# Slot tables filled tile by tile, and expert rows added to the tokens' rows by accumulating scatters, in an encoder layer with 64 experts

## The chip, the cores and the metric

The kernel runs on one core of a Trainium2 chip. The metric is the device time of one execution in microseconds (us), lower is better. The kernel before took 1889.31 us (median of 3 runs, 1889.1 to 1889.86). The execution that the profiler recorded took 1872.73 us, of which 1870.9 us are its span.

## What is computed

One encoder layer on 1024 tokens of width 1024, float32. After the token mixers (a state-space scan and attention, whose outputs are `[s ; a]`), and with alpha = 2^0.25:

```
x1  = LN(alpha * x + [s ; a] @ W_o)
scores = sigmoid(x1 @ w_router); top 6 of 64 experts per token (within the best 4 of 8 groups)
w   = scores of the six / their sum * 2.5
f   = sum over the six of w * ((silu(x1 @ Wg[e]) * (x1 @ Wu[e])) @ Wd[e])  +  the shared expert of x1
out = LN(alpha * x1 + f)
```

Each expert has width 256, so its three weight matrices are 1 MB each. An expert's tokens are handled in blocks of 128 slots. There are 64 main blocks, one per expert, and overflow blocks for experts with more than 128 tokens (here one: the blocks run 65 times).

## The kernel before, in words

The stages run one after another, each in a block with a barrier of all engines behind it. The change touches the last four.

**Mix stage** (`mix_norm_route`, L1022, from 797.9 us of the span). Eight tiles t of 128 tokens. TensorE (PE) makes `[s;a] @ W_o` (L1109, L1114) two tiles ahead, turns x1 (L1123), and makes the router's logits (L1134) and the ranks of the tokens within their experts (L1141, L1143). VectorE (DVE) does the LayerNorm (L1210 to L1223), copies half of the turned x1 (L1265), keeps the ranks (L1259) and picks the experts (L1228 to L1255). SyncE's queue (SP) zeroes the overflow part of `y_d` (24 MB, L1081) and stores x1 rows. The first half of the shared expert's gate and up products (L1005) fills PE's end of the stage.

**Dispatch stage** (`dispatch`, L1292, from about 980 us). DVE computes the overflow blocks and the slot of each of the 8 x 6 x 128 assignments (L1332 to L1358). GpSimd (POOL) then scatters the token numbers with 48 indirect DMAs (L1379) into `slot_tok_d` in memory. SP reads the table back (L1393), PE turns it (L1412), and DVE writes the slot table `block_tok` (L1370). Beside it PE does the shared expert's remaining products (L1005, L1407), DVE adds them to alpha * x1 in `k.x` (L1368), and the first three experts' weights are loaded (ACT's queue, L1322).

**Expert stage** (`moe_experts`, L1422). For each block, in program order on each engine:

- POOL: `gather(e)` copies four index columns (L1485), waits for that copy, and issues four indirect DMAs, one per quarter row (L1489), into one of two `xg` buffers. It waits only for `turn_x(e-2)` (L1497).
- DVE, iteration i: `turn_x(i+2)` (L1614), `hidden(i+1)` (L1619, L1621), `keep_y(i)` (L1631), `keep_hT(i+1)` (L1625).
- PE: `gate_up(c+1)` (L1516), `down(c)` (L1536), `turn_h(c+1)` (L1524).
- ACT: sigmoid (L1572), the other half of `keep_y` (L1578), and the plain store of the block's 128 rows to `y_d` (L1581).
- SP: the three weight loads of expert e+4 when `down(e)` has ended (L1014 to L1016).

**Combine stage** (`combine`, L1672). For each tile POOL gathers six rows per token from `y_d` (L1710, 48 indirect DMAs of 128 rows of 4 KB). Four of them are weighted and added by PE (L1724) and two by DVE (L1755). DVE adds PE's sum (L1758) and does the whole LayerNorm (L1760 to L1770), and SP stores the tile.

The order of the DVE loop is what the prediction leans on:

```
for ii, u:  i = ii * 2 + u
    turn_x(i + 2, u, ...); hidden(i + 1, 1 - u); keep_y(i, u, ...); keep_hT(i + 1, 1 - u)
```

Of the kernel before, what the change touches and what calls it, by code (L numbers as in the profile page):

```python
# [13 lines left out]
P = 128  # L14
# [119 lines left out]
def persistent(nc, ctx, k):  # L134
# [28 lines left out]
    k.y_d = nc.dram_tensor("y_d", (SLOTS, D), f32).ap()  # L163
    k.slot_tok_d = nc.dram_tensor("slot_tok_d", (SLOTS, 1), f32).ap()
# [857 lines left out]
def mix_norm_route(nc, k):  # L1022

    with ExitStack() as ctx:
# [4 lines left out]
        zeros = sb("zeros", [P, D], f32)  # L1029
# [21 lines left out]
        hots = sb("hots", [P, TOP_K, N_EXPERTS], f32)  # L1051
        wsum = sb("wsum", [P, 1], f32)
# [11 lines left out]
        zeroed, y_zeroed = sem("zeroed"), sem("y_zeroed")  # L1064
# [9 lines left out]
        def _(sp):  # L1074
# [16 lines left out]
        def _(pe):
# [34 lines left out]
            def route(t):  # L1126
                pe.wait_ge(xT_dve, t + 1)
# [22 lines left out]
            mix(1)  # L1150
            for t in range(T):
# [8 lines left out]
                if t + 2 >= T:  # L1160

                    n = t + 2 - T
                    pe.wait_ge(mix_read, 2 * t + 2)
                    if n == 0:
                        pe.wait_ge(k.ws_in, 48)
                    shared_gate_up(nc, k, n, p_m[:, n, :]).then_inc(gu_done, 1)
            pe.wait_ge(rank_read, T - 1)
            rank(T - 1)

            pe.wait_ge(rank_read, T)  # L1170
            pe.wait_ge(member_done, T + 1)
# [30 lines left out]
        def _(dve):  # L1202
# [60 lines left out]
            for t in range(T):  # L1263
# [4 lines left out]
                if t:  # L1268
                    keep_rank(t - 1)
# [146 lines left out]

def moe_experts(nc, k):  # L1422
# [423 lines left out]
```

## Time and profile before

| | us |
|---|---|
| median of 3 runs | 1889.31 |
| profiled execution | 1872.73 |
| its span | 1870.9 |
| mixers, up to the mix stage | 798 |
| mix stage | 798 to 980 |
| dispatch stage | 980 to 1059 |
| expert stage | 1059 to 1779 |
| combine stage | 1779 to 1871 |

PE is busy in 87% of the span, DVE in 49%, POOL in 19%, ACT in 18%. Times in rows are microseconds from the span's start, durations are microseconds unless marked ns. A row of the timeline gives start, duration, engine, line, operation, written tile and read tiles, the count, and in brackets the idle time of the engine before it with what ended it. PEclk is TensorE's granted clock as a share of 2.4 GHz.

### The profile page before, as it was taken

How to read it: one execution, taken by the hardware profiler on the slowest of the kernel's cores; microseconds unless marked ns; L12 is line 12 of the kernel's file. 1: busy time of each engine (PE TensorE's matmuls, PEld its weight loads, DVE VectorE, ACT ScalarE, POOL GpSimd, SP SyncE). 2: the span in 40 equal slices, each digit the busy share in tenths (PEclk: the TensorE clock that was granted, in tenths of full speed). 3: DMA queues.
4: the chain of work that ended last, by engine and by line, in shares of the span. 5: the costliest groups of instructions: out<-in, count | busy, mean ns of one | idle time of the engine just before them, and what ended most of it. 6: DMA issues, size and time to landing. Idle time of an engine off the chain costs nothing. (4 is left out here: it accounts for less than half of the span.)

```text
span 1870.9 us, 18631 instructions
## 1 busy us (share of the span) xinstructions
PE 1620.8 (87%) x6004; PEld 929.7 (50%) x6004; DVE 911.0 (49%) x1664; ACT 342.8 (18%) x616; POOL 355.8 (19%) x425
## 2 busy tenths in 40 slices
PE   7989999999665664699989299999999999999775
PEld 4556777777564554245544144444444444444232
DVE  1553444445698884537866133333333333333168
ACT  1303443443412330112200000010100000010010
POOL 0000000000000000000006543333434343343073
PEclk9988999999866666799989699999999999999988
DMA  8010000000411113695008269999999999999296
GB/s 223 12 41 4 4 4 5 5 0 1 42 16 22 19 15 62 230 372 241 35 15 201 97 252 400 401 398 396 395 407 399 394 396 406 397 395 398 104 377 274
DMA packets 117211, 367.34 MB, mean 196 GB/s; under 512 B 38594, under 2 KB 55090, under 8 KB 92210
## 3 DMA queue, kind: packets, MB, share of 16 engines
q1 hardware_dynamic: 84434, 264.00, 39.0%
q0 software_dynamic: 20928, 59.29, 8.1%
q10 hardware_dynamic: 11808, 43.53, 6.6%
q8 instruction: 23, 0.38, 0.1%
q14 instruction: 18, 0.15, 0.0%
HBM read 292.76 MB, written 71.91 MB: 195 GB/s over the span
## 5 line engine op out<-in xcount | busy, mean ns | idle before, releaser
L1516 PE MATMUL moe_p_gu<-ring_gu,moe_xgT 128*128 128x512 f32 x784 | 348.4, 598 | 18.9 <-DVE moe_xgT L1614 18.9
L1489 POOL DMA_INDIRECT moe_xg<-x_d,moe_idx x260 | 247.2, 951 | 114.4 <-issue 63.2
L1516 PEld LDWEIGHTS moe_p_gu<-ring_gu,moe_xgT 128*128 128x128 f32 x784 | 146.9, 192 | 186.4 <-issue 171.1
L1379 POOL DMA_INDIRECT slot_tok_d<-all_const,all_dest_i x48 | 46.5, 970 | 1003.9 <-DVE all_dest_i L1358 989.6
L1536 PE MATMUL moe_p_y<-ring_dn,moe_hT 128*128 128x512 f32 x392 | 176.3, 592 | 0.8 <-DVE moe_hT L1625 0.8
L1619 DVE TENSOR_TENSOR moe_gs<-moe_sig,moe_p_gu 128x256 f32<-128x256 f32 x65 | 27.4, 421 | 303.4 <-ACT moe_sig L1572 303.4
L1614 DVE STREAM_TRANSPOSE moe_xgT<-moe_xg 128x1024 f32<-128x1024 f32 x65 | 131.2, 2020 | 13.0 <-DMA moe_xg<-x_d,moe_idx 11.9
L1572 ACT ACTIVATE moe_sig<-moe_p_gu 128x256 f32<-128x256 f32 x65 | 25.0, 384 | 600.3 <-PE moe_p_gu L1516 600.3
L583 PEld LDWEIGHTS att_p_o<-att_v,att_prT 128*128 128x128 f32 x1024 | 120.4, 192 | 19.5 <-issue 17.6
L583 PE MATMUL att_p_o<-att_v,att_prT 128*128 128x64 f32 x1024 | 123.7, 274 | 1.5 <-DVE att_prT L660 1.5
L530 PE MATMUL att_p_s<-latents_kT,att_qT 96*128 96x512 f32 x256 | 123.6, 607 | 0.0
L646 DVE TENSOR_REDUCE att_nmax<-att_p_s 128x1 f32<-128x1024 f32 x64 | 78.4, 1225 | 92.7 <-PE att_p_s L530 92.4
L1536 PEld LDWEIGHTS moe_p_y<-ring_dn,moe_hT 128*128 128x128 f32 x392 | 74.4, 190 | 94.2 <-issue 94.2
L1631 DVE COPY moe_y<-moe_p_y 128x512 f32<-128x512 f32 x65 | 45.0, 692 | 145.6 <-PE moe_p_y L1536 145.6
L1516 PE MATMUL moe_p_gu<-moe_gu,moe_xgT 128*128 128x512 f32 x256 | 112.5, 592 | 0.0
L753 PE MATMUL ssm_p_v<-ssm_U,ssm_w_in 128*128 x256 | 56.4, 414 | 45.4 <-DVE ssm_gsn L860 31.3
L1724 PE MATMUL comb_p_sum<-comb_yb,comb_diag 128*128 128x512 f32 x128 | 58.7, 613 | 25.0 <-DMA comb_yb<-y_d,all_dest_i 25.0
L753 PEld LDWEIGHTS ssm_p_v<-ssm_U,ssm_w_in 128*128 128x128 f32 x256 | 53.3, 320 | 49.9 <-DVE ssm_gsn L860 34.2
L1516 PEld LDWEIGHTS moe_p_gu<-moe_gu,moe_xgT 128*128 128x128 f32 x256 | 47.5, 191 | 53.6 <-issue 53.6
L616 ACT ACTIVATE att_pr<-att_p_s,att_bias 128x1024 f32<-128x1024 f32 x64 | 71.0, 1110 | 3.1 <-DVE att_bias L647 3.1
L1485 POOL COPY moe_idx<-ring_block_tok 128x4 int32 (+1 forms) x65 | 12.1, 185 | 299.4 <-DVE moe_xgT L1614 291.3
L569 PE MATMUL att_p_t<-all_const,att_pr 128*128 128x128 f32 x512 | 66.9, 274 | 0.0
(319 smaller groups left out, 2178.5 us busy)
## 6 DMA issues: line engine op xcount, KB each, us to landing
ring_gu<-in_we_gate_dram SPq DMA_DIRECT2D x46, 1024.0 KB, 7.9
ring_gu<-in_we_up_dram SPq DMA_DIRECT2D x46, 1024.0 KB, 11.2
ring_dn<-in_we_down_dram SPq DMA_DIRECT2D x46, 1024.0 KB, 13.8
y_d<-moe_y ACTq DMA_DIRECT2D x65, 512.0 KB, 9.3
y_d<-mix_zeros SPq DMA_DIRECT2D x1, 24576.0 KB, 66.2
moe_gu<-in_we_gate_dram SPq DMA_DIRECT2D x16, 1024.0 KB, 8.0
moe_gu<-in_we_up_dram SPq DMA_DIRECT2D x16, 1024.0 KB, 11.3
moe_dn<-in_we_down_dram SPq DMA_DIRECT2D x16, 1024.0 KB, 13.8
```

The costliest lines, as they stand in the source:

```text
L530: last = nc.tensor.matmul(p_s[:, t % 2, half * 512:(half + 1) * 512], qT[:, u, t * P:(t + 1) * P], kT[:, u, half * 512:(half + 1) * 512], ...
L569: last = nc.tensor.transpose(p_t[:, j, :], pr[:, t % 2, j * P:(j + 1) * P], k.ident)
L583: last = nc.tensor.matmul(p_o[:, 0:DV], prT[:, t % 2, j, :], v[:, u, j, :], start=(j == 0), stop=(j == T - 1))
L616: nc.scalar.activation(pr[:, t % 2, :], p_s[:, t % 2, :], ACT.Exp, bias=bias[:, t % 2:t % 2 + 1], scale=SCALE, accum_out=total[:, t % 4:t ...
L646: ch.link(nc.vector.tensor_reduce(nmax[:, t % 2:t % 2 + 1], p_s[:, t % 2, :], AX.X, ALU.max, negate=True))
L753: last = nc.tensor.matmul(p_v[:, x % 2, part, r, :], w_in[:, gd, part * N:part * N + P], U[:, bass.ds(b * GB + half * 4 + r, 1), :].rearra ...
L1379: nc.gpsimd.indirect_dma_start(k.slot_tok_d[:, :], bass.IndirectOffsetOnAxis(ap=k.dest[:, t * TOP_K + q:t * TOP_K + q + 1], axis=0), k.tok ...
L1489: nc.gpsimd.indirect_dma_start(xg[:, u, g, :], None, x1_quarters, bass.IndirectOffsetOnAxis(ap=idx[:, u, g:g + 1], axis=0)).then_inc(xg_in ...
L1516: last = nc.tensor.matmul(p_gu[:, u, :], xgT[:, u, kk, :], k.moe_gu[v][:, :, kk * F:(kk + 1) * F], start=(kk == 0), stop=(kk == KD - 1))
L1536: last = nc.tensor.matmul(p_y[:, half * 512:(half + 1) * 512], hT[:, u, kk, :], k.moe_dn[v][:, kk * D + half * 512:kk * D + (half + 1) * 512],
L1614: nc.vector.transpose(xgT[:, u].rearrange("p k (g i) -> p g k i", g=NQ), xg[:, u].rearrange("p g (j k) -> p g k j", k=KD)).then_inc(x_turn ...
L1724: last = nc.tensor.matmul(p_sum[:, t % 2, cols], diag[:, t % 2, q, :], yb[:, n % NB, cols], start=(q == 0), stop=(q == PE_K - 1))
```

## The change

- **Slots.** A slot is now (level, expert, place): level = rank // 128 takes the place of the compacted overflow number, so a tile's destinations (`place(t)`) are known as soon as its ranks are. They are scattered in the mix stage, tile by tile, as entries of three numbers: token for the gather, token for the scatter, weight. Unfilled slots hold token number 1024 + place and weight 0.
- **Mix stage.** POOL adds the LayerNorm's bias (`shift`) and issues the 48 scatters. ACT copies the whole turned x1. All four parts of the shared expert's gate and up products are made here. The stage ends with the tables' way back: 64 blocks by a plain load, the 48 overflow blocks by an indirect one, then six transposes.
- **No dispatch stage.** The shared expert's down products and the sum with alpha * x1 move to the start of the expert stage, and SP stores the sums to `sum_d`.
- **Expert stage.** POOL copies three small tables per block, gathers with a bounds check, and issues for each block one indirect DMA that adds the 128 weighted rows (4 KB each) to `sum_d`. It does so once the block's rows are in `y` and the scatter before it has landed. The weighting is in the two copies from PSUM.
- **Combine stage.** Eight plain loads of `sum_d`, statistics, normalisation on ACT, scale on DVE, bias on POOL, store.

The diff, cut to its core:

```diff
@@ mix_norm_route
+            def shift(t):
+                pool.wait_ge(scaled, t + 1)
+                nc.gpsimd.tensor_tensor(k.x[:, t, :], r[:, :], b1[:, :], ALU.add).then_inc(x1_done, 1)
+            def scatter(t):
+                pool.wait_ge(dest_done, t + 1)
+                for q in range(TOP_K):
+                    n = t * TOP_K + q
+                    nc.gpsimd.indirect_dma_start(k.slot_d[:, :], bass.IndirectOffsetOnAxis(ap=k.dest[:, n:n + 1], axis=0),
+                                                 k.entry[:, t, q, :], None).then_inc(scattered, 16)
...
             for t in range(T):
                 turn_x(t)
                 if t + 3 < T:
                     turn_o(t + 3)
                 if t + 2 < T:
                     mix(t + 2)
+                else:
+                    pe.wait_ge(mix_read, 2 * t + 2)
+                    shared(t + 2 - T)
                 if t:
                     rank(t - 1)
                 route(t)
+            shared(2)
             pe.wait_ge(rank_read, T - 1)
             rank(T - 1)
...
+            shared(3)
+            pe.wait_ge(main_in, 16)
+            pe.wait_ge(over_in, 16)
...
+            def place(t):
                 dve.wait_ge(ranked, t + 1)
-                nc.vector.tensor_copy(k.rank[:, t, :], p_rank).then_inc(rank_read, 1)
+                nc.vector.tensor_tensor(hots[:, :, :], hot[:, :, :], p_rank.unsqueeze(1).to_broadcast([P, TOP_K, N_EXPERTS]),
+                                        ALU.mult).then_inc(rank_read, 1)
+                dve.wait_ge(rank_read, t + 1)
+                ch.link(nc.vector.tensor_reduce(rank[:, :], hots[:, :, :], AX.X, ALU.add))
...
             for t in range(T):
-                dve.wait_ge(x_turned, 2 * t + 1)
-                nc.vector.tensor_copy(k.x1T[:, 0:4, t * P:(t + 1) * P], p_x[:, 0:4, :]).then_inc(xT_dve, 1)
                 if t + 1 < T:
                     norm(t + 1)
                 if t:
-                    keep_rank(t - 1)
+                    place(t - 1)
                 route(t)
@@ moe_experts
+            for t in range(T):
+                sp.wait_ge(s_read, 2 * t + 2)
+                sp.dma_start(k.sum_d[t * P:(t + 1) * P, :], k.x[:, t, :]).then_inc(sum_out, 16)
...
+            def gather(n, col, u, c, free=None):
+                if free is not None:
+                    pool.wait_ge(x_turned, free)
+                nc.gpsimd.tensor_copy(dst[:, c, :], k.block_dst[:, bass.ds(col, 1)]).then_inc(idx_done, 1)
+                nc.gpsimd.tensor_copy(wgt[:, c, :], k.block_w[:, bass.ds(col, 1)]).then_inc(idx_done, 1)
+                nc.gpsimd.tensor_copy(idx[:, u, :], k.block_tok[:, bass.ds(col, 1), :].rearrange("p b g -> p (b g)")).then_inc(idx_done, 1)
+                pool.wait_ge(idx_done, n * 3 + 3)
                 pool.sem_inc(idx_seen, 1)
                 for g in range(NQ):
                     nc.gpsimd.indirect_dma_start(xg[:, u, g, :], None, x1_quarters,
-                                                 bass.IndirectOffsetOnAxis(ap=idx[:, u, g:g + 1], axis=0)).then_inc(xg_in[u], 16)
+                                                 bass.IndirectOffsetOnAxis(ap=idx[:, u, g:g + 1], axis=0),
+                                                 bounds_check=NQ * SEQ - 1, oob_is_err=False).then_inc(xg_in[u], 16)
+            def scatter(n, u, c, first=False):
+                pool.wait_ge(y_act, n + 1)
+                pool.wait_ge(y_dve, n + 1)
+                if not first:
+                    pool.wait_ge(y_out, n * 16)
+                pool.sem_inc(y_taken, 1)
+                nc.gpsimd.indirect_dma_start(k.sum_d[:, :], bass.IndirectOffsetOnAxis(ap=dst[:, c, :], axis=0),
+                                             y[:, u, :], None, compute_op=ALU.add).then_inc(y_out, 16)
...
+            gather(2, OVER + 2, 0, 2, free=1)
+            pool.wait_ge(sum_out, 16 * T)
+            scatter(0, 0, 0, first=True)
+            gather(3, OVER + 3, 1, 3, free=2)
+            scatter(1, 1, 1)
+            with pool.Fori(0, E // 4 - 1) as ee:
+                for v in range(4):
+                    e = ee * 4 + v
+                    gather(e + 4, ee * 4 + (OVER + 4 + v), v % 2, v, free=e + 3)
+                    scatter(e + 2, v % 2, (v + 2) % 4)
...
-            def keep_y(e, u, n):
+            def keep_y(e, u, c, sent=True):
                 dve.wait_ge(y_done, e * 2 + 2)
-                if n is not None:
-                    dve.wait_ge(y_out[u], n)
-                nc.vector.tensor_copy(y[:, u, 512:D], p_y[:, 512:D]).then_inc(y_dve, 1)
+                if sent:
+                    dve.wait_ge(y_out, e * 16 - 16)
+                nc.vector.tensor_scalar(y[:, u, 512:D], p_y[:, 512:D], wgt[:, c, :], None, ALU.mult).then_inc(y_dve, 1)
...
-            with dve.Fori(1, E // 2 - 1) as ii:
-                for u in range(2):
-                    i = ii * 2 + u
-                    turn_x(i + 2, u, ii * LANDED + 2 * LANDED, i + 1)
+            with dve.Fori(0, E // 4 - 1) as ii:
+                for v in range(4):
+                    i, u = ii * 4 + v + 2, v % 2
+                    turn_x(i + 2, u, ii * (2 * LANDED) + (v // 2 + 3) * LANDED, i + 1)
                     hidden(i + 1, 1 - u)
-                    keep_y(i, u, ii * 16)
+                    keep_y(i, u, (v + 2) % 4)
                     keep_hT(i + 1, 1 - u)
@@ combine
+            for t in range(T):
+                sp.dma_start(k.x[:, t, :], k.sum_d[t * P:(t + 1) * P, :]).then_inc(x_in[t], 16)
...
+                nc.gpsimd.tensor_tensor(xn[:, t, :], xn[:, t, :], b2[:, :], ALU.add).then_inc(out_done, 1)
...
+                nc.scalar.activation(xn[:, t, :], k.x[:, t, :], ACT.Identity, bias=nbias[:, t:t + 1], scale=rstd[:, t:t + 1]).then_inc(normed, 1)
```

## Rows read from the trace of the kernel before

**Rows 1.** Busy time by stretch: start:end, length, then each engine's busy time, clock, DMA.

```profile
1250.00:1350.00 100.00, 100.00 (x249) 45.55 (x248) 37.17 (x48) 9.43 (x19) 36.24 (x47) 1.00 1.01 399
```

**Rows 2.** The timeline of one expert block in the steady part.

```profile
1304.47 7.03 PE L1516 MATMUL moe_p_gu<-ring_gu,moe_xgT 128*128 128x512 f32 x16
1304.53 0.69 DVE L1631 COPY moe_y<-moe_p_y 128x512 f32<-128x512 f32 x1 [2.23 <-PE moe_p_y L1536]
1305.47 2.02 DVE L1614 STREAM_TRANSPOSE moe_xgT<-moe_xg 128x1024 f32<-128x1024 f32 x1
1307.66 0.18 POOL L1485 COPY moe_idx<-ring_block_tok 128x4 int32 x1 [4.93 <-DVE moe_xgT L1614]
1308.63 0.97 POOL L1489 DMA_INDIRECT moe_xg<-x_d,moe_idx  x1 [0.79 <-POOL moe_idx L1485]
1309.90 0.95 POOL L1489 DMA_INDIRECT moe_xg<-x_d,moe_idx  x1 [0.30 <-issue]
1311.34 3.60 PE L1536 MATMUL moe_p_y<-ring_dn,moe_hT 128*128 128x512 f32 x8
1311.95 0.42 DVE L1619 TENSOR_TENSOR moe_gs<-moe_sig,moe_p_gu 128x256 f32<-128x256 f32 x1 [4.46 <-ACT moe_sig L1572]
1312.41 0.42 DVE L1621 TENSOR_TENSOR moe_h<-moe_gs,moe_p_gu 128x256 f32<-128x256 f32 x1
```

**Rows 3.** Tile moe_xg, 1250 to 1350 us: from a gather's issue to its landing.

```profile
DMA to landing us min/median/max: 4.9/6.3/7.1
```

**Rows 4.** Tile moe_xg, 1080 to 1095 us, when few other transfers run.

```profile
DMA to landing us min/median/max: 2.7/2.8/2.9
```

**Rows 5.** DMA over 1150 to 1700 us: bytes and rate.

```profile
DMA packets 40082, 219.05 MB, mean 398 GB/s; under 512 B 6668, under 2 KB 6668, under 8 KB 20024
```

**Rows 6.** DMA issues: KB each, median us to landing (1730 to 1780; 1780 to 1871).

```profile
y_d<-moe_y ACTq DMA_DIRECT2D x4, 512.0 KB, 2.6
comb_yb<-y_d,all_dest_i POOLq DMA_INDIRECT x48, 9.1
```

**Rows 7.** Timeline: expert stage, first product, first and last copies of its chain, end.

```profile
1072.56 9.07 PE L1516 MATMUL moe_p_gu<-ring_gu,moe_xgT 128*128 128x512 f32 x16 [15.02 <-DVE moe_xgT L1614]
1093.86 0.69 DVE L1631 COPY moe_y<-moe_p_y 128x512 f32<-128x512 f32 x1 [2.14 <-PE moe_p_y L1536]
1736.12 0.69 DVE L1631 COPY moe_y<-moe_p_y 128x512 f32<-128x512 f32 x1 [2.14 <-PE moe_p_y L1536]
1755.35 8.82 PE L1516 MATMUL moe_p_gu<-ring_gu,moe_xgT 128*128 128x512 f32 x16 [3.92 <-DVE moe_xgT L1614]
1779.21 0.35 SPq L1693 DMA_DIRECT2D comb_g<-in_ln_g_dram  x1
```

**Rows 8.** Groups of instructions from 950 to 1065 us (busy us, mean ns).

```profile
L1379 POOL DMA_INDIRECT slot_tok_d<-all_const,all_dest_i x48 | 46.5, 970 | 1003.9 <-DVE all_dest_i L1358 989.6 <-issue 14.3
L1407 PE MATMUL disp_p_y<-shared_dn,shared_hT 128*128 128x512 f32 x64 | 27.6, 592 | 0.0
```

**Rows 9.** Timeline of the mix stage: one tile, and PE in the last two.

```profile
879.46 0.22 DVE L1259 COPY all_rank<-mix_p_o 128x64 f32<-128x64 f32 x1 [0.21 <-PE mix_p_o L1143]
881.50 0.23 DVE L1228 TENSOR_TENSOR mix_choice<-mix_score,mix_r_bias 128x64 f32<-128x64 f32 x1 [1.82 <-ACT mix_score L1196]
895.30 1.22 DVE L1223 TENSOR_TENSOR all_x_sb<-mix_r,mix_b 128x1024 f32<-128x1024 f32 x1
898.32 1.09 PE L1123 MATMUL mix_p_x<-all_const,all_x_sb 128*128 128x128 f32 x8
932.44 1.10 PE L1123 MATMUL mix_p_x<-all_const,all_x_sb 128*128 128x128 f32 x8
963.01 13.95 PE L1005 MATMUL mix_p_m<-shared_x1T,shared_gu 128*128 128x512 f32 x32
```

**Rows 10.** Tile all_x_sb, 1780 to 1871 us: min/median/max ns, first and last start.

```profile
L1755 DVE SCALAR_TENSOR_TENSOR all_x_sb<-comb_yb,all_top_w,all_x_sb x16: 1277/1283/1286, 1792.4 to 1859.8; 128x1024 f32<-128x1024 f32 x16
L1769 DVE TENSOR_TENSOR all_x_sb<-all_x_sb,comb_g x8: 1224/1226/1227, 1799.5 to 1865.4; 128x1024 f32<-128x1024 f32 x8
```

More of the change, by code:

```diff
@@ L1196, in _ @@
                 nc.scalar.activation(score[:, t % 2, :], p_log, ACT.Sigmoid).then_inc(score_done, 1)
-            for n in range(KF):
-                act.wait_ge(gu_done, n + 1)
-                nc.scalar.activation(sig[:, n, :], p_m[:, n, 0:512], ACT.Sigmoid).then_inc(sig_done, 1)
+                if t + 2 >= T:
+                    gate(t + 2 - T)
+            gate(2)
+            gate(3)
         @block.vector
@@ new lines, in _ @@
+                if t == T - 1:
+                    dve.sem_inc(member_done, 1)
+                    hidden(0)
+            hidden(1)
+            place(T - 1)
+            dve.wait_ge(ranked, T + 1)
+            ch.link(nc.vector.tensor_scalar(over[:, :], p_rank, float(P), None, ALU.is_gt))
+            for m in range(2, LEVELS):
+                ch.link(nc.vector.scalar_tensor_tensor(over[:, :], p_rank, float(P * m), over[:, :], ALU.is_gt, ALU.add))
+            ch.link(nc.vector.tensor_tensor_scan(over_end[:, :], k.ones[:, 0:N_EXPERTS], over[:, :], 0.0, ALU.mult, ALU.add))
@@ new lines, in _ @@
+            gather(E, 0, 0, 0, free=E - 1)
+            scatter(E - 2, 0, 2)
+            scatter(E - 1, 1, 3)
+            n_over = pool.value_load(k.n_over[0:1, 0:1], min_val=0, max_val=OVER)
+            with pool.If(n_over > 0):
+                scatter(E, 0, 0)
+            for j in range(1, 4):
+                with pool.If(n_over > j):
+                    gather(E + j, j, j % 2, j, free=E + j - 1)
+                    scatter(E + j, j % 2, j)
+            with pool.Fori(1, OVER // 4) as round_, pool.If(n_over > round_ * 4):
+                for v in range(4):
+                    j = round_ * 4 + v
@@ L1545, in step @@
                 turn_h(n, c + 1)
+            for n in range(2 * T):
+                t, cols = n // 2, slice(n % 2 * 512, (n % 2 + 1) * 512)
+                if n >= 2:
+                    pe.wait_ge(s_read, n - 1)
+                for f in range(KF):
+                    last = nc.tensor.matmul(p_s[:, n % 2, :], k.s_hT[:, f, t * P:(t + 1) * P], k.ws_dn[:, f, cols],
+                                            start=(f == 0), stop=(f == KF - 1))
+                last.then_inc(s_done, 1)
             gate_up(0, 0)
@@ L1583, in _ @@
             gate(0, 0)
             gate(1, 1)
-            keep_y(0, 0, None)
+            keep_y(0, 0, 0, sent=False)
             gate(2, 0)
-            keep_y(1, 1, None)
-            with act.Fori(1, E // 2 - 1) as ii:
-                for u in range(2):
-                    i = ii * 2 + u
-                    gate(i + 1, 1 - u)
-                    keep_y(i, u, ii * 16)
+            keep_y(1, 1, 1, sent=False)
+            with act.Fori(0, E // 4 - 1) as ii:
+                for v in range(4):
+                    i = ii * 4 + v + 2
+                    gate(i + 1, (v + 1) % 2)
+                    keep_y(i, v % 2, (v + 2) % 4)
```

540 lines of the change are left out of this document (232 added, 308 removed).

## The prediction

> **What bounds the kernel now.** I read the busy times by stretch first, then the timeline of one expert block, then the two stages around the expert stage. In the expert stage PE is busy 100.00 of 100.00 us at the full granted clock, and the DMA engines are as full (share 1.01) [rows 1]. A block is PE work and nothing else: 7.03 us of gate and up products, 3.60 us of down products, two short transposes [rows 2]. From the first `keep_y` (ends 1094.55) to the one 61 blocks later (ends 1736.81) each block takes 642.3 / 61 = 10.53 us [rows 7]. All else hides under that. A gather issued at 1308 to 1313 has landed by about 1319 and is used near 1326.5, two blocks after the `turn_x` of 1305.47 [rows 2, 3]. The transfers move 398 GB/s [rows 5], some 4.2 MB a block: 3.15 of weights, 0.52 gathered, 0.52 stored.
>
> The dispatch stage is bound by POOL: 48 scatters at 1.26 us (970 ns busy, 0.30 between) make 61 us, and PE's shared products lie beneath them [rows 8]. The combine stage is bound by DVE, a tile every 9.4 us [rows 10].
>
> **The expert block's new period.** This decides the outcome. POOL's new program order is gather(e+3), scatter(e+1), gather(e+4). The scatter waits for `keep_y(e+1)`, so gather(e+4) can't be issued before that copy is done, though its buffer has been free for long. On DVE, `turn_x(e+4)` comes right behind `keep_y(e+1)` and `keep_hT(e+2)`, and behind `turn_x(e+4)` stand `hidden(e+3)` and then `keep_y(e+2)`, which lets the next scatter go. So one loop is closed once per block: keep_y, scatter, gather, turn_x, hidden, keep_y. Its length:
>
> - DVE's end to the scatter's start, with a semaphore step as before the first gather: 0.8 (rows show 0.79 for the step and 0.17 for a bare wake-up, from `turn_x`'s end at 1307.49 to 1307.66) [rows 2].
> - The scatter on POOL: 0.97, as the first gather of a group [rows 2].
> - Three index copies of 0.18 in place of one: 0.54; then the step to the first gather: 0.79 [rows 2].
> - The fourth gather starts three spacings later, 3 x 1.27 = 3.8 [rows 2].
> - Its landing L: 2.8 us when little else moves [rows 4], 6.3 us in the full stage [rows 3].
> - `turn_x` 2.02 + 0.05, `hidden` 2 x 0.42 + 0.08, `keep_y` 0.69 + 0.03: 3.7 [rows 2].
>
> That is 10.6 + L: 13.4 with the light landing, 16.9 with the full one, 12.8 with the light landing and the bare wake-up. All are above 10.53. For L, at a period of 14.3 the DMA engines have some 4.7 MB to move (the accumulate reads its 0.52 MB of rows too), 330 GB/s or 0.83 of the 398. The weight loads start when `down` ends, about 4 us before the loop's copy, and are mostly gone when the fourth gather goes. So I take L near the light row, a quarter of the way up: 3.7, period **14.3 us**. The loop closes between keep_y(0) and keep_y(61): 61 x (14.3 - 10.53) = **+230 us**. Bounds: 12.8 gives +138, 16.9 gives +389.
>
> By the Trainium skill (DMA: Bandwidth & Descriptors, Anatomy of one DMA — SWDGE (gpsimd) path), a DMA of this kind takes about 2.0 us plus its bytes at 436 GB/s, an estimate of 2.3 us for a quarter gather; the period would be 12.9 and the change +60 us, not +145. Rows 4 show 2.7 at the least, with few transfers beside.
>
> The bounds check and the adding scatter show nowhere in this trace. The check lies from 0 (the gathers' 0.95 us is the same work) to one more gather's 0.95 us per gather; I take 0 and keep the rest in the range. Skipped rows (some 6144 of 8192 slots of the main blocks are filled) could shorten a landing, at most to the 2.7 of rows 4. The scatter's landing lies between 2.6 us, a plain store of the same rows alone, and twice the 9.1 us of a gather of 4 KB rows in the crowded combine [rows 6]. Only above some 13 us would it set the period through its own wait on the scatter before; I take less.
>
> PE will idle 3.8 us a block. The idle 3.92 us ahead of 1755.35 was followed by a product of 8.82 us in place of 7.03, so part of it ran at 1.2 GHz [rows 7]. That makes 10.53 + 1.8 = 12.3, still under 14.3: no cost.
>
> **Ahead of the loop: -29 us.** DVE per tile in the mix stage loses the turned copy (0.69) and the bias (1.22), and gains `place`, about 2.2 us of small operations. These fit in the rank copy's 0.22 and the 1.82 us that it waits for the scores [rows 9]. The bias on POOL is on the way to PE's `turn_x`: DVE would be done near 894.8 and PE wants x1 at 898.32 [rows 9], so 3.5 us are free. The bound below is DVE's 1.22 for it; up to 3.5 it costs nothing, at 5 it would cost 1.5 on each of seven tiles. I take 0. The 48 scatters (six, 7.6 us, per tile of 17.3) lie beside; only the last six show. ACT's wider copy has slack. Stores and zeroing change nothing here: the x1 stores stood behind 24 MB of zeros on SP's queue and now stand behind 0.8 MB.
>
> The stage's end is a row of PE work with two waits. From the transposes of tile 6 (932.44 [rows 9]), PE does shared(0), 14 us [rows 9], ranks and logits 2.6, transposes 1.1, shared(1) 14, ranks and logits 2.6: 967.7. Then shared(2) waits for `hidden(0)`, which stands on DVE behind `route(7)` (7.4 us from the scores) and ends at 977. Shared(2) with 1.2 us of slow clock ends at 992.5, shared(3) at 1008. Beside the latter, place(7) ends at 996.5, POOL's last six scatters at 1004, landed at 1007, tables read by 1010, turned and copied with `hidden(3)` by 1014.5. In the expert stage 64 down products follow, 27.6 us [rows 8] and 1.7 of slow clock, so the first gate and up product starts at 1044 where it was 1072.56 [rows 7]. POOL's scatter(0) waits for the stores of the sums, which stand behind 12.6 MB of weights on SP's queue: 16.8 MB and two gathers at 398 GB/s from 1015 land near 1060, about when `keep_y(0)` does (1065, before 1094.55 [rows 7]). -29; later landings could cost 10.
>
> **Behind the loop: -56 us.** From keep_y(61) to the combine stage nothing changes (42.4 us [rows 7]). The combine stage took 91.7 us (1779.21 [rows 7] to the end). Now: the first load lands after 2.6 [rows 6], DVE has 1.7 of statistics, 0.4 of small ones and 1.23 of scale [rows 10] per tile, 3.4 x 8 = 27, then bias and store 1.2 + 2.6: 34 to 36. POOL's bias becomes the bound only above 3.4 us a tile.
>
> **Sum.** +230 - 29 - 56 = +145 us on the profiled 1872.7 (span 1870.9 and 1.8 around), 2018. The runs' median is 16.6 us above that execution; the forecast in their terms is 1889.3 + 145 = **2034 us**.
>
> **Rivals.**
>
> - *The loop is not closed* (0.05): the gathers still land in time and the period stays 10.53. Then only the two stages count: 1889.3 - 85 = 1804, faster. For it: before, gathers had 7 us to spare. Against it: the order on POOL and DVE above, which no slack changes. It decides below a period of 10.53 + 85 / 61 = 11.9, that is with keep_y to landing in 8.2 us, where the shortest rows give 9.1.
> - *The adding scatter is slow, or the gathers stand behind it in POOL's queue* (0.15): both are in one queue. With L = 6.3 [rows 3] the period is 16.9, 1889.3 + 304 = 2193. With a landing of 9.1 [rows 6] it is 19.7, 2363.
> - *PE stays at 1.2 GHz* (0.03): a block of 21.1 us, 1889.3 + 645 - 85 = 2449. Against it: the first product, after 15.02 us of idling, took 9.07 and not 14, and the one after 3.92 took 8.82, so the clock came back within each [rows 7]. The Trainium skill (TensorE: Matmul & The Clock Gate, Part 1) has the clock fall after idling and come back under sustained work; by that each block would start slow and end fast, as in rows 7.
>
> **How the numbers follow.** The forecast case has 0.77. Its own range is 1942 (12.8) to about 2193. For 8 in 10 I leave out its ends, the slow clock and most of the slow scatter: 1945 to 2165. What a measurement can tell from no change here is 0.2%, about 4 us. Slower 0.94, same 0.01, faster 0.05.
>
> **What would show it.** In the expert stage PE should idle about 3.8 us a block, most of it ahead of L1524's transposes on DVE's `hidden`; DVE's longest wait should be `turn_x` on the gathers' landing; POOL's on `keep_y`. The DMA share should fall to 0.8. The first product should start near 1044, the combine stage take about 35 us. It is wrong if `keep_y` comes every 10.6 us, or if POOL waits for the scatter's landing instead.

## The result and the profile after

The changed kernel takes **2096.7 us** (median of 4 runs, 2093.9 to 2098.0) where the kernel before takes 1889.6 on the same chip (4 runs, 1889.1 to 1893.2): ratio 1.109, 95% interval 1.107 to 1.111. The profiled execution took 2097.95 us, span 2096.1, against the 1872.73 and 1870.9 of before: the two spans differ by 225.2 us. The medians, from one chip, differ by 207.1 us. The profiled execution of before lies 16 us under its runs on that chip, so the 225.2 that is split below holds some difference between chips too.

The costliest groups of the changed kernel, from its page (busy and mean ns, then the idle time before them and who ended it):

```profile
L1634 DVE STREAM_TRANSPOSE moe_xgT<-moe_xg 128x1024 f32<-128x1024 f32 x65 | 131.2, 2019 | 689.1 <-DMA moe_xg<-x_d,moe_idx 687.8
...
L1490 POOL DMA_INDIRECT sum_d<-moe_y,moe_dst x65 | 105.5, 1623 | 492.9 <-DVE moe_y L1651 457.8
L1542 PE MATMUL moe_p_h<-all_const,moe_h 128*128 128x128 f32 x130 | 37.3, 378 | 197.6 <-DVE moe_h L1641 197.5
```

DVE waited 688 us for gathers to land, POOL 458 us for `keep_y`, PE 198 us for `hidden` ahead of its short transposes. That is a ring of waits, and a single stretch of the expert stage shows what it does to the engines [rows 1]:

```profile
1400.00:1500.00 100.00, 82.35 (x179) 35.69 (x179) 23.31 (x32) 7.51 (x14) 42.87 (x56) 0.90 0.82 275
```

PE works 82 of 100 us, at a mean granted clock of 0.90, and the transfers fall from 399 to 275 GB/s. Two blocks of the steady part, from the timeline [rows 2]:

```profile
1500.88 0.33 SPq L1013 DMA_DIRECT2D moe_gu<-in_we_gate_dram  x1
...
1507.16 0.74 DVE L1651 TENSOR_SCALAR moe_y<-moe_p_y,moe_wgt 128x512 f32<-128x512 f32 x1
...
1507.30 0.70 PE L1542 MATMUL moe_p_h<-all_const,moe_h 128*128 128x128 f32 x2 [6.58 <-DVE moe_h L1641]
...
1507.90 9.70 PE L1534 MATMUL moe_p_gu<-moe_gu,moe_xgT 128*128 128x512 f32 x16
...
1508.87 1.63 POOL L1490 DMA_INDIRECT sum_d<-moe_y,moe_dst  x1 [8.99 <-DVE moe_y L1651]
...
1509.94 0.76 POOL L1473 COPY moe_dst<-shared_block_dst 128x1 int32 x1
...
1511.79 1.05 POOL L1479 DMA_INDIRECT moe_xg<-x_d,moe_idx  x1 [0.86 <-POOL moe_idx L1475]
...
1515.78 1.00 POOL L1479 DMA_INDIRECT moe_xg<-x_d,moe_idx  x1 [0.30 <-issue]
...
1517.44 3.60 PE L1554 MATMUL moe_p_y<-moe_dn,moe_hT 128*128 128x512 f32 x8
...
1518.66 2.03 DVE L1634 STREAM_TRANSPOSE moe_xgT<-moe_xg 128x1024 f32<-128x1024 f32 x1 [10.20 <-DMA moe_xg<-x_d,moe_idx]
...
1521.20 0.33 SPq L1013 DMA_DIRECT2D moe_gu<-in_we_gate_dram  x1
1521.37 0.74 DVE L1651 TENSOR_SCALAR moe_y<-moe_p_y,moe_wgt 128x512 f32<-128x512 f32 x1
...
1521.85 7.03 PE L1534 MATMUL moe_p_gu<-moe_gu,moe_xgT 128*128 128x512 f32 x16
...
1523.08 1.62 POOL L1490 DMA_INDIRECT sum_d<-moe_y,moe_dst  x1 [6.31 <-DVE moe_y L1651]
...
1529.97 1.00 POOL L1479 DMA_INDIRECT moe_xg<-x_d,moe_idx  x1 [0.30 <-issue]
...
1534.94 2.01 DVE L1634 STREAM_TRANSPOSE moe_xgT<-moe_xg 128x1024 f32<-128x1024 f32 x1 [12.47 <-DMA moe_xg<-x_d,moe_idx]
...
1537.62 0.74 DVE L1651 TENSOR_SCALAR moe_y<-moe_p_y,moe_wgt 128x512 f32<-128x512 f32 x1
```

Read it as one chain: `keep_y` 1507.16, scatter 1508.87, gathers 1511.79 to 1515.78, `turn_x` 1518.66, `keep_y` 1521.37, and again to 1537.62. The two blocks take 14.21 and 16.25 us. They differ in one link, from the start of the fourth gather's issue to `turn_x`: 2.88 and 4.97 us. Such pairs repeat through the whole stage.

The ends of the chain, from the timeline [rows 7]:

```profile
1047.37 7.03 PE L1534 MATMUL moe_p_gu<-moe_gu,moe_xgT 128*128 128x512 f32 x16
...
1066.63 0.75 DVE L1651 TENSOR_SCALAR moe_y<-moe_p_y,moe_wgt 128x512 f32<-128x512 f32 x1 [2.14 <-PE moe_p_y L1554]
...
1998.39 0.74 DVE L1651 TENSOR_SCALAR moe_y<-moe_p_y,moe_wgt 128x512 f32<-128x512 f32 x1
...
2012.31 0.75 DVE L1651 TENSOR_SCALAR moe_y<-moe_p_y,moe_wgt 128x512 f32<-128x512 f32 x1 [2.14 <-PE moe_p_y L1554]
...
2020.89 1.57 POOL L1490 DMA_INDIRECT sum_d<-moe_y,moe_dst  x1 [5.40 <-DMA sum_d<-moe_y,moe_dst]
...
2036.74 0.75 DVE L1651 TENSOR_SCALAR moe_y<-moe_p_y,moe_wgt 128x512 f32<-128x512 f32 x1 [4.16 <-PE moe_p_y L1554]
...
2052.38 4.17 SPq L1713 DMA_DIRECT2D all_x_sb<-sum_d  x8
...
2058.07 0.69 DVE L1748 BATCH_NORM_STATS2 comb_stats<-all_x_sb 128x6 f32<-128x512 f32 x1 [20.58 <-DMA all_x_sb<-sum_d]
```

From `keep_y(0)` to `keep_y(61)`: 931.8 us, 15.27 a block, where it was 10.53. The 225.2 us split without rest (to rounding): up to the end of `keep_y(0)` -27.2, over 61 blocks +289.5, behind `keep_y(61)` -37.1 (134.1 before, 97.0 now).

### The profile page after: what moved, and what is told of

It reads as the page before. It is cut to its first block and busy times, and to the rows that moved or that the text cites. A ratio compares the mean times of both kernels' runs of the same rounds, so it can differ in the third digit from the quotient of the medians.

```text
span 2096.1 us, 18608 instructions
## 1 busy us (share of the span) xinstructions
PE 1654.8 (79%) x5878; PEld 927.2 (44%) x5878; DVE 856.1 (41%) x1634; ACT 352.4 (17%) x592; POOL 486.7 (23%) x590
## 3 DMA queue, kind: packets, MB, share of 16 engines
q10 hardware_dynamic: 1440, 1.05, 0.2%
## 5 line engine op out<-in xcount | busy, mean ns | idle before, releaser
L1534 PE MATMUL moe_p_gu<-moe_gu,moe_xgT 128*128 128x512 f32 x1040 | 537.0, 676 | 4.3 <-DVE moe_xgT L1634 4.3
L1534 PEld LDWEIGHTS moe_p_gu<-moe_gu,moe_xgT 128*128 128x128 f32 x1040 | 223.6, 221 | 276.3 <-issue 276.3
L1554 PE MATMUL moe_p_y<-moe_dn,moe_hT 128*128 128x512 f32 x520 | 233.9, 592 | 1.8 <-DVE moe_hT L1645 1.8
L1490 POOL DMA_INDIRECT sum_d<-moe_y,moe_dst x65 | 105.5, 1623 | 492.9 <-DVE moe_y L1651 457.8
L1542 PE MATMUL moe_p_h<-all_const,moe_h 128*128 128x128 f32 x130 | 37.3, 378 | 197.6 <-DVE moe_h L1641 197.5
L1554 PEld LDWEIGHTS moe_p_y<-moe_dn,moe_hT 128*128 128x128 f32 x520 | 98.6, 190 | 125.5 <-issue 124.4
L1542 PEld LDWEIGHTS moe_p_h<-all_const,moe_h 128*128 128x128 f32 x130 | 20.9, 205 | 247.3 <-DVE moe_h L1641 246.3
L752 PE MATMUL ssm_p_v<-ssm_U,ssm_w_in 128*128 x256 | 53.3, 397 | 46.2 <-DVE ssm_gsn L859 30.3
L1004 PE MATMUL mix_p_m<-mix_x1T,mix_gu 128*128 128x512 f32 x128 | 58.3, 615 | 9.5 <-DVE shared_hT L1337 9.5
L620 ACT ACTIVATE att_prT<-att_p_t 128x512 f32<-128x512 f32 x64 | 38.2, 597 | 138.5 <-PE att_p_t L568 138.5
L1603 ACT ACTIVATE moe_y<-moe_p_y,moe_wgt 128x512 f32<-128x512 f32 x65 | 44.7, 688 | 97.4 <-PE moe_p_y L1554 97.4
## 6 DMA issues: line engine op xcount, KB each, us to landing
all_x_sb<-in_x_dram SPq DMA_DIRECT2D x8, 512.0 KB, 12.3
```

The lines of the kernel that those rows point to most:

```text
L752: last = nc.tensor.matmul(p_v[:, x % 2, part, r, :], w_in[:, gd, part * N:part * N + P], U[:, bass.ds(b * GB + half * 4 + r, 1), :].rearra ...
L1004: last = nc.tensor.matmul(sums[:, part * 512:(part + 1) * 512], k.ws_gu[:, kk, part * F + f * P:part * F + (f + 1) * P], k.x1T[:, kk, half ...
L1490: nc.gpsimd.indirect_dma_start(k.sum_d[:, :], bass.IndirectOffsetOnAxis(ap=dst[:, c, :], axis=0), y[:, u, :], None, compute_op=ALU.add).th ...
L1534: last = nc.tensor.matmul(p_gu[:, u, :], xgT[:, u, kk, :], k.moe_gu[v][:, :, kk * F:(kk + 1) * F], start=(kk == 0), stop=(kk == KD - 1))
L1554: last = nc.tensor.matmul(p_y[:, half * 512:(half + 1) * 512], hT[:, u, kk, :], k.moe_dn[v][:, kk * D + half * 512:kk * D + (half + 1) * 512],
```

## The experiments

The kernel before took 1870.1 us on the chip of the first four experiments, 1890.7 on that of the next four, 1870.6 on that of the last four; its time differs by chip, so ratios are against before on the same chip. The changed kernel itself was timed only beside the 1889.6, so where a run is set against it, that is across chips, and the period is the safer figure. e3 to e7 are single executions. "Period" is the mean from `keep_y(0)` to `keep_y(61)`, read from each profile's timeline. Where nothing else is said, the edit is to the changed kernel.

**e1, copies ahead.** The three index copies are taken off the path from scatter to gathers.

```diff
-                    gather(e + 4, ee * 4 + (OVER + 4 + v), v % 2, v, free=e + 3)
+                    issue(e + 4, v % 2)
+                    keep_dst(ee * 4 + (OVER + 4 + v), v)
+                    prep(ee * 4 + (OVER + 5 + v), (v + 1) % 2, (v + 1) % 4, e + 4)
```

> The changed kernel, with the weight and index copies of a gather put ahead of the scatter on GpSimd and the destination copy behind the gathers. Theory (one loop per block: keep_y, scatter, gather, turn_x, hidden, keep_y): in the changed kernel the first gather starts 2.92 us after the scatter; now it should start 0.30 after the scatter's 1.63, at 1.93, so each of 61 blocks is 1.0 us shorter: about 2097 - 61 = 2036 us, period 15.28 to 14.3. Rival (the DMA queue, or the landing of the adding scatter, sets the period): the copies are not on the path, the time stays within 5 us of 2097.

2096.15 us, ratio 1.121 (1.119 to 1.122), period 15.23: within 1 us of the changed kernel, and the period stayed (15.27 there). The closed-loop theory in its first form missed by 60 us. Two blocks of its timeline:

```profile
1506.61 9.73 PE L1561 MATMUL moe_p_gu<-moe_gu,moe_xgT 128*128 128x512 f32 x16
...
1509.52 1.04 POOL L1492 DMA_INDIRECT moe_xg<-x_d,moe_idx  x1 [0.31 <-issue]
...
1516.37 2.03 DVE L1661 STREAM_TRANSPOSE moe_xgT<-moe_xg 128x1024 f32<-128x1024 f32 x1 [9.20 <-PE moe_p_gu L1561]
...
1519.91 0.75 DVE L1678 TENSOR_SCALAR moe_y<-moe_p_y,moe_wgt 128x512 f32<-128x512 f32 x1 [0.76 <-PE moe_p_y L1581]
...
1527.52 1.00 POOL L1492 DMA_INDIRECT moe_xg<-x_d,moe_idx  x1 [0.30 <-issue]
...
1533.69 2.01 DVE L1661 STREAM_TRANSPOSE moe_xgT<-moe_xg 128x1024 f32<-128x1024 f32 x1 [12.70 <-DMA moe_xg<-x_d,moe_idx]
```

The first gather now starts 1.95 us behind the scatter (1507.57 to 1509.52) and not 2.92, as the edit meant. But in the short block `turn_x` and `keep_y` wait for PE, whose gate and up products took 9.73 us, part of them at the lower clock; and in the long one the gathers take 6.17 us from the last issue to `turn_x` in place of 4.97. So two more limits lie close behind the chain: the landing beside the weight loads, and PE at its lower clock.

**e2, the order opened.** Each scatter is issued one block later than in the changed kernel: the gather of block e+4 stands behind the scatter of block e and no longer behind that of e+1, so it no longer waits for the newest `keep_y`.

```diff
-                    gather(e + 4, ee * 4 + (OVER + 4 + v), v % 2, v, free=e + 3)
-                    scatter(e + 2, v % 2, (v + 2) % 4)
+                    gather_ahead(e + 4, col, v % 2, v, e + 3)
+                    scatter_behind(e + 1, (v + 1) % 2, (v + 1) % 4, col, v)
```

> The changed kernel with gather(e+4) ahead of scatter(e+1) on GpSimd, so that no gather waits for a keep_y. Theory: the loop is open and the period falls by at least 3 us a block; below it lies the next bound, TensorE's 10.53 or the DMA engines (per block of the changed kernel the weight queue has 53.0% and GpSimd's queue 26.7% of 15.28 us on the 16 engines, 12.2 us together). Between 10.53 and 12.2 the time is 2097 - 61 x (15.28 - P) = 1807 to 1909; I expect P near 11.8, 1885 us. Rival (the adding scatter itself is what is slow, by its landing of about 7 us and its place in the queue): the time stays above 2030.

**1843.34 us, ratio 0.985 (0.984 to 0.987)**: 1.5% faster than before, and 252.8 us under e1, which has the closed order and ran on the same chip. The period is 11.15; 61 x (15.23 - 11.15) = 249 us, nearly the whole difference. The order of POOL's program is the cause. What is left over 10.53 shows in the DMA queues from 1150 to 1700 us (packets, MB, share of 16 engines) and in one of the waits there:

```profile
q1 hardware_dynamic: 21203, 154.42, 69.4%
q0 software_dynamic: 16461, 45.45, 33.3%
...
sum_d<-moe_y,moe_dst POOLq DMA_INDIRECT x50, 10.3
```

```profile
POOL moe_dst L1497 <- DMA sum_d<-moe_y,moe_dst: 130.4, 49, 3.6
```

The engines' shares sum to 1.03, but before they made 1.01 with PE at 100% [rows 1], so the share alone does not tell what limits. The scatter lands 10.3 us after its issue, and in every block POOL waits for that landing, 2.7 us; e9 comes back to it.

**e3, a plain store in place of the add**, in the closed order (it leaves out the sum over a token's experts): `compute_op=ALU.add` is taken out.

> The changed kernel with the order unchanged and the scatter storing the rows instead of adding them (the sum over experts is left out: the last writer's row stays). Theory: the loop stays closed, so most of the 4.75 us a block stay; what the add costs shows as the scatter's issue (1.63 us, to 0.97 if the add is the cause: -0.66 us a block, -40 us) and as shorter landings of the gathers behind it in the queue (-0.5 to -1 us a block). Period 14.1 at most 14.6, time 2020 to 2060. Rival (the add's engine time is the cause of the slowdown): period below 12, time below 1910.

2053.64 us, period 14.56. POOL's part of the scatter is 1.02 us and the copies behind it run in 0.19 each:

```profile
1505.91 1.02 POOL L1490 DMA_INDIRECT sum_d<-moe_y,moe_dst  x1 [6.29 <-DVE moe_y L1651]
...
1506.94 0.19 POOL L1473 COPY moe_dst<-shared_block_dst 128x1 int32 x1
```

With the add it is 1.63 and 0.76. The add costs 0.7 us a block on the chain; it is not what closes the loop.

**e4, few loads**: the loads of the main blocks' weights are cut to 64 columns each (it leaves most of the expert weights unread).

> The changed kernel with the weights of experts 4 and up loaded only in their first 64 columns (the rest of the ring keeps old weights, so the outputs of those experts are wrong by that), order unchanged. The weight traffic is gone from the expert stage. Theory: the loop alone, without contention: every gather lands in 2.1 to 2.8 us, the alternation of 14.0 and 16.6 us per block is gone, all blocks take 13.6 to 14.1; time 2097 - 61 x 1.4 = 2010 (1995 to 2025). Rival (the period is DMA bandwidth): without the weights it falls to TensorE's 10.53, time near 1810.

1999.95 us, period 13.77, and the alternation is gone: blocks take 13.4 to 14.8 us in no fixed order. From the trace of tile moe_xg, 1200 to 1700 us:

```profile
DMA to landing us min/median/max: 2.1/2.8/3.9
```

And from its timeline, PE's last short transposes of a block and the product behind them:

```profile
1504.48 0.51 PE L1551 MATMUL moe_p_h<-all_const,moe_h 128*128 128x128 f32 x2 [2.58 <-DVE moe_h L1650]
...
1504.82 7.03 PE L1543 MATMUL moe_p_gu<-moe_gu,moe_xgT 128*128 128x512 f32 x16
```

With little beside them the gathers land in 2.8 us [rows 4], and the bare chain of POOL and DVE is 13.8 us. The product shown is at full speed, but not all are: of 19 gate and up products behind 2.3 to 4.1 us of idling (1200 to 1700 us), 14 took 8.2 to 9.9 us and 5 took 7.03. They did not hold the chain: from 1150 to 1700 us DVE waited for PE once, 0.6 us. The other 1.5 of the 15.27 comes with the weights being moved at the same time.

**e5, e1 and e4 together** (the weights unread as in e4).

> Two edits together: the index copies made one block ahead (as e1) and weight loads of 64 columns in the main blocks (as e4; it leaves the expert weights unread). Theory (in the kernel after, the alternate long blocks are held by gathers landing late among the weight loads, and the pure chain of keep_y, scatter, gathers, turn_x, hidden holds the rest): without the loads the copies are on the path again, so the 1.0 us that e1 took from scatter to first gather must show in full: keep_y every 12.8 us where e4 had 13.77, time 1.0 x 61 = 60 us under e4, near 1940. Rival (the copies are free whatever else runs, because PE at half clock or the scatter's own wait holds the block): period 13.8 as in e4, time near 2000.

1952.90 us, period 12.85: 0.92 under e4. The copies are worth their microsecond where the chain is the only limit, and gave nothing in e1, where its timeline shows loads and PE's clock close behind. Few loads also shorten PE's idle stretches, so e5 does not tell those two apart.

**e6, gate and up loads early.** SP asks for block e's gate and up weights after the gate and up products of block e-4, not after its down products.

```diff
+                    load_gate_up(sp, k, v, e)
                     sp.wait_ge(y_done, e * 2 - (2 * RING - 2))
-                    load_expert(sp, k, v, e)
+                    load_down(sp, k, v, e)
```

> After, with the gate and up loads of block e+3 issued as soon as the gate and up products of block e have read their buffer, 3.6 us ahead of the down load; all transfers stay. Theory (long blocks come from gathers, adding scatter and 3.15 MB of weights asked for at once): two thirds of the weights move out of the gathers' way, the long blocks shrink from 16.6 to 14.5 to 15.5, mean period 14.2 to 15.0, time 2030 to 2080. Rival (the long blocks come from something else, as the adding scatter's read and write): period 15.27 and time 2097 as after.

2088.62 us, period 15.17, long blocks of 16.4 as before. The timeline shows that the edit did not do what it was meant to:

```profile
1521.32 0.33 SPq L1020 DMA_DIRECT2D moe_dn<-in_we_down_dram  x1
...
1521.96 0.33 SPq L1013 DMA_DIRECT2D moe_gu<-in_we_gate_dram  x1
```

PE does gate and up of the next block ahead of down of this one, so their buffer was free early, but on SP's queue the loads stood behind the down load of the block before, and all three still went out together at the end of a down product. It says nothing on whether spreading them would help; that stays open.

**e7, e2's order with a plain store** (the sum left out as in e3).

> The order of e2 (scatter one block later, gather ahead of it) with the scatter storing in place of adding; it leaves out the sum of a token's rows. Theory (with the loop open the expert stage is bound by the bytes and engine time of the DMA queues, of which the adding scatter takes more than a plain one): q0 share falls from 33 to about 22 percent, period from 11.15 to 10.5 to 10.8, POOL's wait on the scatter's landing gone, time 1805 to 1825. Rival (what is left above 10.53 is POOL's order, not the add): period 11.1, time 1843 as e2.

1804.57 us, period 10.53, PE 200.00 of 200.00 us busy from 1200 to 1400. The queues there, 1150 to 1700 us:

```profile
q1 hardware_dynamic: 22567, 164.30, 78.5%
q0 software_dynamic: 17642, 48.45, 22.0%
```

Share times period gives engine time a block for queue 0: 0.333 x 11.15 = 3.71 us in e2, 0.220 x 10.53 = 2.32 here. The add takes 1.4 us more of all 16 engines than the store. With it both queues together make 1.03 x 11.15 = 11.5 us a block, over PE's 10.53. That is no bare need, though: for the same bytes the weights' queue has 0.694 x 11.15 = 7.7 us in e2 and 0.785 x 10.53 = 8.3 here. Of the 4.74 us that the change added to a block, 4.1 come from the order (e2 alone gets them back) and the last 0.6 from the add.

**e8, e2 with unfilled slots skipped** by `bounds_check=SEQ - 1, oob_is_err=False` on the adding scatter.

> The order of e2, and the adding scatter skips the rows of unfilled slots by a bounds check (about a quarter of them), output the same. Theory (the adding scatter's bytes are what the open loop waits for): a quarter of its engine time goes, period 10.8 to 11.0, time 1825 to 1840, ratio 0.976 to 0.984. Rival (unfilled rows cost nothing now since they all hit one place, or a skipped row costs as much as a moved one): 1843 as e2, ratio 0.985.

1852.52 us, ratio 0.980 (0.978 to 0.981), period 11.34. The ratio falls where the theory wanted it, but the period is over e2's 11.15, and the chips differ by 20 us in before. A ratio carries the chip, too: e11, the same kernel but for two small edits, takes 1848.59 us on another chip, 4 us less, and has 0.988. e11 decides.

**e9, e2 with the copy behind the scatter.**

```diff
-                keep_dst(col, v)
                 nc.gpsimd.indirect_dma_start(k.sum_d[:, :], bass.IndirectOffsetOnAxis(ap=dst[:, c, :], axis=0),
                                              y[:, u, :], None, compute_op=ALU.add).then_inc(y_out, 16)
+                keep_dst(col, v)
```

> The order of e2, with the copy of the scatter's index column made behind the adding scatter and not between the landing of the scatter before and it. In e2 POOL waits 2.7 us a block for the scatter before it to have landed, then spends 0.18 and 0.50 us on that copy, then issues: scatter, landing, copy, scatter is a loop of its own. Theory (that loop sets e2's 11.15 us): the period falls by 0.4 to 0.7 us, to 10.5 to 10.8, time 20 to 40 us under e2 on the same chip. Rival (the DMA engines are full, share 1.02, and bytes set 11.15): period 11.1, time as e2.

1841.99 us, ratio 0.984 (0.983 to 0.986); e12 beside it 1843.09. Period 11.12 against 11.17. From the waits, 1150 to 1700 us:

```profile
POOL sum_d L1508 <- DMA sum_d<-moe_y,moe_dst: 150.5, 47, 3.6
```

```profile
sum_d<-moe_y,moe_dst POOLq DMA_INDIRECT x49, 10.3
```

```profile
1503.43 1.62 POOL L1508 DMA_INDIRECT sum_d<-moe_y,moe_dst  x1 [3.50 <-DMA sum_d<-moe_y,moe_dst]
...
1514.82 1.61 POOL L1508 DMA_INDIRECT sum_d<-moe_y,moe_dst  x1 [3.52 <-DMA sum_d<-moe_y,moe_dst]
```

The forecast gain did not come, but this does not refute the second loop, because the edit hardly touched it. From a scatter's landing to the next scatter's start pass 0.91 us in e12 (0.87 to 0.96, 17 blocks between 1200 and 1400 us) and 0.80 in e9 (0.76 to 0.85): the 0.5 us behind the copy did not go away with it, it is now booked as waiting, 3.2 us in place of 2.7. Only 0.1 us left the loop, and the landing is 10.3 us against 10.2. Landing and step make 10.3 + 0.8 = 11.1 us, the period, and each scatter is released by the landing of the one before. So the loop of scatter and landing closes in every block, and what sets the period is the length of the landing. It is 6.2 us with few loads (e4) and 10.3 here. Whether full engines, the place in the queue or the add itself make it so long, these runs do not separate.

**e10, e9 with the last two biases of the combine stage on VectorE.**

```diff
-                nc.vector.tensor_tensor(xn[:, t, :], xn[:, t, :], g2[:, :], ALU.mult).then_inc(scaled, 1)
+                    ch.link(nc.vector.tensor_tensor(xn[:, t, :], xn[:, t, :], g2[:, :], ALU.mult))
+                    nc.vector.tensor_tensor(xn[:, t, :], xn[:, t, :], b2[:, :], ALU.add).then_inc(tail_done, 1)
```

> As e9, and in the combine stage the bias of the last two tiles is added by VectorE right behind its own scale and not by GpSimd. In the kernel after, a VectorE operation with two operands in SBUF that starts beside GpSimd's 2.34 us add ends only when that does (2.33 in place of 0.16, 3.32 in place of 1.23 us), and the last add is GpSimd's. Theory: the scale of the last tiles is back at 1.2 us, and the span ends 2 to 4 us earlier than e9's. Rival (the long operations have another cause, as the landing of stores): the scale of the last tile still takes about 3.3 us, span as e9's within 1 us.

**1836.43 us, ratio 0.982 (0.980 to 0.983)**, the best version found. The end of e9's timeline, then that of e10:

```profile
1827.52 2.34 POOL L1756 TENSOR_TENSOR comb_xn<-comb_xn,comb_b 128x1024 f32<-128x1024 f32 x1 [1.23 <-DVE comb_xn L1791]
1827.55 2.32 DVE L1787 SCALAR_TENSOR_TENSOR comb_nbias<-comb_mv,comb_rstd 128x1 f32<-128x1 f32 x1
...
1831.09 2.34 POOL L1756 TENSOR_TENSOR comb_xn<-comb_xn,comb_b 128x1024 f32<-128x1024 f32 x1 [1.23 <-DVE comb_xn L1791]
1831.18 3.33 DVE L1791 TENSOR_TENSOR comb_xn<-comb_xn,comb_g 128x1024 f32<-128x1024 f32 x1 [0.17 <-ACT comb_xn L1762]
```

```profile
1824.84 2.33 DVE L1790 SCALAR_TENSOR_TENSOR comb_nbias<-comb_mv,comb_rstd 128x1 f32<-128x1 f32 x1
...
1829.48 1.22 DVE L1797 TENSOR_TENSOR comb_xn<-comb_xn,comb_g 128x1024 f32<-128x1024 f32 x1
1830.73 1.22 DVE L1798 TENSOR_TENSOR comb_xn<-comb_xn,comb_b 128x1024 f32<-128x1024 f32 x1
```

The last scale is 1.22 and not 3.33 once POOL adds nothing beside it. From the last long `comb_nbias` to the span's end e9 takes 12.5 us (1827.55 to 1840.0) and e10 10.2 (1824.84 to 1835.0): 2.3 us are this edit's. The rest of the 5.6 between the medians is not explained by it; in the two profiles 2.7 us lie ahead of the first `keep_y` (1066.92 and 1064.22), where the kernels are alike.

**e11, e10 with unfilled slots skipped.**

> As e10, and the adding scatter skips unfilled slots by a bounds check. Theory (what is left of the wait on the scatter's landing is the rows that it moves): landing shorter, period lower than e10 by 0.1 to 0.5 us, time 5 to 30 us lower on the same chip. Rival (landing does not depend on these rows, or the check costs as much as it spares, as e8 with 11.34 beside e2's 11.15 on another chip hints): same as e10 within 4 us or up to 12 us slower.

1848.59 us, ratio 0.988 (0.987 to 0.990), 12 us over e10 on the same chip; period 11.31 against 11.11, and 61 x 0.20 = 12: the whole difference is in the period. The scatter lands after 10.4 us (10.2 in e10) though it moves fewer rows, queue 0's share falls from 33.6 to 29.5%, and the whole moves 348 GB/s in place of 365. Fewer bytes and a longer block: the rival holds. The landing, not the bytes, goes with the period here as in e9. Why skipped rows do not shorten it, no run here shows.

**e12, e2 again.**

> e2 once more, for the comparison on this chip. All theories: ratio to before 0.975 to 0.985, period 11.0 to 11.4.

1843.09 us, ratio 0.986 (0.984 to 0.987), period 11.17.

## Why the prediction was right, and where its terms were off

**The loop** was called as it is: order on POOL and DVE closes it, and undoing the order alone (e2) brings the period to 11.15, 61 x 4.12 = 251 us. The DMA share was put at 0.8 and is 0.82, in part by luck: the forecast came from 4.7 MB a block at 330 GB/s, and the profile counts 275 GB/s, which at 15.27 us is 4.2 MB, without the rows that the add was taken to read. The period was put at 14.3 and is 15.27 over 61 blocks; the two blocks above, mean 15.23, show which terms were short:

- `keep_y`'s end to the scatter: 0.8 taken, 0.97 measured (1507.16 + 0.74 to 1508.87). +0.17.
- Scatter, copies and step: 0.97 + 0.54 + 0.79 = 2.30 taken, 2.92 measured. This is the worst term. The adding scatter keeps POOL 1.63 us, not a gather's 0.97, and the copies run partly under it at 0.75 each; e3 shows that the add does both. +0.62.
- Three spacings: 3.8 taken, 3.99. The gather with a bounds check takes 1.00 to 1.05 in place of 0.95 [rows 2]. +0.19.
- Landing: 3.7 taken, 2.88 and 4.97, mean 3.92. The mean was nearly right, but by luck: it is a mixture of two cases. When PE has idled 6.58 us its products take 9.70, the down product ends late, and the next weight loads are asked for at 1521.20, beside `keep_y`; they are under way when the gathers follow at 1526 to 1530. In the other blocks they go out 5 to 6 us ahead of `keep_y` (1500.88 against 1507.16) and are mostly gone, as the prediction had it. +0.22. That the loads are what makes the gathers late is shown by e4; that PE's clock sets the alternation is read from the timeline, not tried.
- `turn_x`, `hidden`, `keep_y`: 3.7 taken, 2.70 + 0.74 = 3.44. -0.26.

Together +0.94 on 14.3. Over 61 blocks the loop cost 289.5 where 230 stood. Against the profiled execution the sum said 2018 and it took 2097.95: 80 us short, 60 in the loop, 2 in the head, 19 in the tail. Against the medians (2034 and 2096.7) it is 63, because the 16.6 us between the median of before and its profiled execution have no counterpart after (2096.7 and 2097.95).

**PE's clock** was costed at nothing by 10.53 + 1.8 = 12.3. PE idles 3.0 us a block in the mean (198 / 65), but not evenly: 4.4 to 6.6 us in about every second block and little in the others. The product behind the long stretch takes up to 9.9 us, not 8.8. PE's own row, 0.7 + 9.7 + 3.6 = 14.0, is then just under the 14.2 of the short block; in 6 of 36 blocks `keep_y` already waited for PE, 0.5 us at most. No cost was right by a hair, and e1 ran into it at once. The Trainium skill (TensorE: Matmul & The Clock Gate, Part 1) has the clock fall after idling and come back under work; the trace agrees, with 9.70 us behind 6.58 us of idling and 7.03 in the next block, behind 0.47. How long a stretch costs is not fixed in these runs: behind 2.6 us e4 has both 7.03 and 8.73.

**The head**: -27.2 against -29. The first product starts at 1047.37, forecast 1044. In the working shared(3) should end at 992.5 + 14 = 1006.5 and not 1008, which moves nothing, as the tables come later.

**The tail**: -37.1 against -56, the second term that failed. The combine stage takes 43.7 us (2052.4 to 2096.1), forecast 35. The first sum arrives 5.7 us after its issue and not 2.6; eight loads go out together, but that this is the reason was not tried. A tile takes 3.57 us and not 3.4: its `comb_nbias` takes 0.70 us beside POOL's add in place of 0.16. In the last tile `comb_nbias` (2.33) and the scale (3.32) are held by that add, and e10 gets 2.3 us of it back. Ahead of it the prediction had "nothing changes", and it grew from 42.4 to 53.3 us (1999.13 to 2052.38). `keep_y(62)` came 13.9 us after the one before it, not 10.5, since the closed order still holds there. From the end of the last `keep_y` (2037.49) to the loads of the sums pass 14.9 us where before had 7.9 (1771.36 to 1779.21): the last adding scatter has to be issued and to land. That landing was in none of the terms.

**The add's landing** was said to matter only above 13 us. In the closed loop it set nothing in the main blocks (the wait at 2020.89 comes behind them); it is 6.2 us with few loads (e4) and 10.3 in the open order. The rival "the adding scatter is slow" was thus wrong as a bound of the changed kernel and right for the version without the loop, where the scatter's landing and the step to the next scatter make the period (e9).

**The lower bound from the page** (the Trainium skill, DMA: Bandwidth & Descriptors, Anatomy of one DMA — SWDGE (gpsimd) path: an estimate of 2.3 us for a quarter gather) is too low here: 2.8 median with almost no other transfers in e4, where some landed in 2.1.

## What to carry to other kernels

When an operation that waits for the newest result is put on an in-order queue ahead of the prefetch, the prefetch is no longer one: walk the ring of waits through every engine's program order and sum it, and compare the sum with the period of the engine that bounds now. Here the way back was the order of two calls (251 us). A ring that hides under another limit gives nothing back until that limit moves too, so an edit without gain (e1) doesn't prove that the term is free; take the neighbour away and try again (e5). And before an edit is said to refute a ring, read from its trace how much it took off that ring: e9 took off 0.1 us where 0.5 was meant.

## What the runs showed of the hardware

- An adding indirect scatter of 128 rows of 4 KB holds POOL for 1.63 us, a plain one for 1.02 (e3); together with four gathers it takes 3.7 us of all 16 DMA engines in e2 and 4.6 in e4, with the plain one 2.3 in e7 and 2.4 in e3. It lands after 6.2 us with few other transfers (e4) and 10.3 in the open order (e2). Copies on POOL issued behind it take 0.75 in place of 0.19.
- Skipping unfilled rows, about a quarter, by a bounds check did not shorten its landing (10.4 us against 10.2) and made the kernel 12 us slower (e11 against e10).
- A VectorE operation with two operands in SBUF that starts beside POOL's 2.34 us tensor_tensor does its work only when that has ended: 2.32 in place of 0.16 us, and 3.33 in place of 1.22, which ends 1.08 us behind the add; operations with one operand (the statistics, 0.68) are not held. The Trainium skill (SBUF — State Buffer, SBUF: two separate sides) states this lock; the trace agrees, and e10 shows it by taking POOL's add away.
- The kernel before takes 1870 us in two of the four sets of runs and 1890 in the two others, each on its chip, though within a set it repeats within 0.4%; the profile that the prediction went by was taken at 1872.7. The changed versions do not show this gap (e8 and e11, nearly alike, 1852.5 and 1848.6 us). So neither times nor ratios of two chips are set against each other without a look at the period.
